# Three first weight chunks side by side instead of two, in a kernel that computes one hybrid attention and pooling layer

## What is computed

```
h = einsum('bsd,de->bse', x, w_in)                       # 2048 -> 9216 + 1024 + 1024 + 1024 + 4096
q, k, v, z_attn, u_pool, z_pool, g_pre = split(h, ...)
y_attn = (softmax-combined dilated attention of q, k, v) * silu(z_attn)
y_pool = causal_pool_mixer(u_pool, w_pool, pool_scale) * silu(z_pool)
merged = sigmoid(g_attn) * (y_attn @ w_proj_attn) + sigmoid(g_pool) * (y_pool @ w_proj_pool)
return layer_norm(2 ** 0.25 * x + merged @ w_out, ln_gamma, ln_beta)
```

## Time and profile before

| what | value |
|---|---|
| median of 3 runs | 961.87 us (961.44 to 961.93) |
| the profiled execution, its own time | 960.2 us |
| its span (first to last instruction) | 958.4 us |
| PE busy | 947.3 us, 99% of the span |
| PE weight loads (beside the matmuls) | 838.7 us |
| DVE busy | 633.7 us, 66% |
| ACT busy | 423.2 us, 44% |
| moved from HBM | 174.87 MB |

### The profile page before, as it was taken

One profiled execution on the slowest core, in us unless ns is written; L12 is line 12 of the kernel. 1 busy time (PEld: TensorE's weight loads), 2 busy tenths in 40 slices (PEclk: granted clock), 3 DMA queues, 4 the chain that ended last, 5 costly groups with the idle time before them and its releaser, 6 DMA issues.

```text
span 958.4 us, 14944 instructions
## 1 busy us (share of the span) xinstructions
PE 947.3 (99%) x5346; PEld 838.7 (88%) x5346; DVE 633.7 (66%) x996; ACT 423.2 (44%) x592; POOL 0.2 (0%) x4
## 2 busy tenths in 40 slices
PE   8999999999999999999999999999999999999996
PEld 6998898898898898898898899888888888888884
DVE  6767567567567567567567568666666666665666
ACT  6454354354354354354354354545445444543330
POOL 0000000000000000000000000000000000000000
PEclk9999999999999999999999999999999999999998
DMA  8744454445444445544444445655555554555532
GB/s 320 283 176 176 176 176 176 175 175 175 175 175 175 176 174 175 175 175 175 177 173 175 176 174 219 221 178 210 182 178 197 186 183 177 213 204 196 182 126 88
DMA packets 27543, 177.24 MB, mean 185 GB/s; under 512 B 3455, under 2 KB 4223, under 8 KB 7039
## 3 DMA queue, kind: packets, MB, share of 16 engines
q1 hardware_dynamic: 26928, 173.53, 50.1%
q10 hardware_dynamic: 596, 3.45, 1.0%
HBM read 174.87 MB, written 2.10 MB: 185 GB/s over the span
## 4 chain that ended last, share of the span: by engine, by line
PE 96%; DVE 1%; DMA 1%; SPq 1%; issue 0%; ACT 0%; DVEq 0%
PE proj_ps L337 40%; PE proj_ps L338 20%; PE attn_ps L337 6%; PE attn_ps L331 4%; PE attn_ps L332 4%; PE attn_ps L333 4%; PE attn_ps L338 3%; PE value_ps L332 3%; PE value_ps L333 3%; PE value_ps L331 3%; PE mixed_ps L445 1%; DMA w_raw<-in_weights 1%; PE mixed_ps L331 1%; PE mixed_ps L333 1%; PE mixed_ps L332 1%; PE attn_ps L406 1%
## 5 line engine op out<-in xcount | busy, mean ns | idle before, releaser
L337 PE MATMUL proj_ps<-xt,w_hi 128*128 128x512 f32 x1664 | 586.9, 397 | 1.8 <-DVE w_lo L756 1.0
L338 PE MATMUL proj_ps<-xt,w_lo 128*128 128x256 f32 x1664 | 466.9, 281 | 0.0
L727 DVE TENSOR_TENSOR w_lo<-w_raw,w_hi 128x1024 fp32r<-128x1024 f32 x318 | 374.2, 1220 | 81.5 <-ACT w_hi L576 80.1
L337 PEld LDWEIGHTS proj_ps<-xt,w_hi 128*128 128x128 f32 x1664 | 312.9, 188 | 76.3 <-DVE xt L749 1.5
L576 ACT ACTIVATE w_hi<-w_raw 128x1024 fp32r<-128x1024 f32 x318 | 318.3, 1051 | 54.1 <-PE mixed_ps L333 27.1
L338 PEld LDWEIGHTS proj_ps<-xt,w_lo 128*128 128x128 f32 x1664 | 315.0, 189 | 0.0
L595 ACT ACTIVATE corr<-proj_ps 128x256 f32<-128x256 f32 x104 | 39.9, 384 | 288.0 <-PE proj_ps L338 288.0
L741 DVE TENSOR_TENSOR qk_f<-proj_ps,corr 128x256 f32<-128x256 f32 x48 | 20.3, 424 | 79.0 <-ACT corr L595 79.0
L337 PE MATMUL attn_ps<-yp,w_hi 128*128 128x512 f32 x128 | 45.9, 397 | 0.0
L337 PE MATMUL attn_ps<-ya,w_hi 128*128 128x512 f32 x128 | 45.6, 396 | 0.0
L331 PE MATMUL attn_ps<-w_hi,xt 128*128 128x384 f32 x128 | 42.9, 335 | 0.0
(11 more groups left out here) (151 smaller groups left out, 884.4 us busy)
## 6 DMA issues: line engine op xcount, KB each, us to landing
w_raw<-in_weights SPq DMA_DIRECT2D x158, 1024.0 KB, 4.8
res<-in_x_rows ACTq DMA_DIRECT2D x1, 2048.0 KB
out_rows<-res SPq DMA_DIRECT2D x8, 256.0 KB, 2.2
xt_raw<-in_xt SPq DMA_DIRECT2D x3, 512.0 KB, 6.7
w_raw<-in_weights SPq DMA_DIRECT2D x6, 256.0 KB, 6.5
w_raw<-in_weights SPq DMA_DIRECT2D x2, 512.0 KB, 9.2
gamma<-in_gamma_row ACTq DMA_DIRECT2D x1, 1024.0 KB
mask<-in_mask SPq DMA_DIRECT2D x1, 576.0 KB, 4.4
```

The source lines that it names most:

```text
L337: mm(bank, w_hi[:, slot, cols], tile.rearrange("p a s -> p (a s)"), start=first, stop=False)
L338: return mm(bank[:, SEQ:2 * SEQ], w_lo[:, slot, cols], tile[:, 0, :], start=False, stop=last)
L727: tt(w_lo[:, slot, cols], w_raw[:, slot, cols], w_hi[:, slot, cols].bitcast(F32), ALU.subtract).then_inc(lo_split, 1)
```

## The change

PE works on chunks 0, 1 and 2 side by side, in bank 0 of `proj_ps`, in `value_ps` and in `mixed_ps` (both are first written otherwise much later in head 0). The weights of all three land in four pieces of four k-tiles; x keeps its five pieces. SP issues a piece of x and then the same piece of chunks 0, 1 and 2, where before the whole of chunk 2 came last. ACT issues three transfers of 256 KB in place of two of 128 KB. ACT and DVE split the pieces in the same order. In head 0, `next_bank` is left out for j = 0 to 2, and the split of chunk 2 is gone from the loop's lead-in. There are 11 warm-up matmuls instead of 8. The corresponding edits on DVE (`x_lo_part`, the loop over three chunks, the bank as an argument of `halves_summed`) mirror those on ACT.

```
-WARM_UP = 8
-
-PIECES = ((0, 2), (2, 4), (4, 8), (8, 12), (12, 16))
+WARM_UP = 11
+
+X_PIECES = ((0, 2), (2, 4), (4, 8), (8, 12), (12, 16))
+PIECES = ((0, 4), (4, 8), (8, 12), (12, 16))
+LAST = len(PIECES) - 1
...
+        def first_bank(n):
+
+            return (proj_ps[:, 0, :], value_ps[:, :], mixed_ps[:, :])[n]
+
+        def bank_of(j, first):
+            return first_bank(j) if first and j < RING else proj_ps[:, j % 2, :]
+
...
-        x_landed = [sem(f"x_landed{q}") for q in range(len(PIECES))]
+        x_landed = [sem(f"x_landed{q}") for q in range(len(X_PIECES))]
...
-        piece_landed = [[sem(f"piece_landed{n}_{q}") for q in range(len(PIECES) - 1)] for n in range(2)]
-        half_landed = sem("half_landed")
+        piece_landed = [[sem(f"piece_landed{n}_{q}") for q in range(LAST)] for n in range(RING)]
...
             load_x(0)
             load_x(1)
-            load_piece(0, 1)
-            load_piece(1, 1)
-            for q in range(2, len(PIECES)):
-                load_x(q)
-                load_piece(0, q)
-                load_piece(1, q)
-            for half, signal in enumerate((half_landed, raw_landed[2])):
-                cols = slice(half * HALF * P, (half + 1) * HALF * P)
-                sp.dma_start(w_raw[:, 2, cols], stream_d[2, :, cols]).then_inc(signal, 16)
+            for q in range(1, len(PIECES)):
+                load_x(q + 1)
+                for n in range(RING):
+                    sp.dma_start(w_raw[:, n, piece_cols(q)], stream_d[n, :, piece_cols(q)]).then_inc(
+                        piece_arrival(n, q), 16)
...
                 for q, (before, upto) in enumerate(PIECES):
-                    pe.wait_ge(x_lo_done, q + 1)
-                    for n in range(2):
+                    for n in range(RING):
                         if q == LAST:
                             pe.wait_ge(lo_split, 2 * n + 2)
                         else:
-                            pe.wait_ge(piece_lo_done, 2 * q + n + 1)
+                            pe.wait_ge(piece_lo_done, RING * q + n + 1)
                         for k in range(before, upto):
-                            bank, tile, first, last = from_x(n)(k)
-                            done = k_tile(bank, tile, n, k, first, last)
+                            x_piece = [start for start, _ in X_PIECES]
+                            if n == 0 and k in x_piece:
+
+                                pe.wait_ge(x_lo_done, x_piece.index(k) + 1)
+                            done = k_tile(first_bank(n), xt[:, k, :, :], n, k, k == 0, k == KT - 1)
...
-                    if first and j < 2:
+                    if first and j < RING:
                         if j == 0:
                             first_chunks()
...
-                    next_bank(0, j, i)
+                    if not first or j >= RING:
+                        next_bank(0, j, i)
...
-            for n in range(2):
+            for n in range(RING):
                 act.dma_start(w_raw[:, n, piece_cols(0)], stream_d[n, :, piece_cols(0)]).then_inc(
                     piece_landed[n][0], 16)
...
-            for q, (before, upto) in enumerate(PIECES):
+            def x_hi_part(q):
+                k = slice(*X_PIECES[q])
                 act.wait_ge(x_landed[q], 16)
-                activation(xt[:, before:upto, 0, :], xt_raw[:, before:upto, :], ACT.Copy).then_inc(x_hi_done, 1)
-                for n in range(2):
+                activation(xt[:, k, 0, :], xt_raw[:, k, :], ACT.Copy).then_inc(x_hi_done, 1)
+
+            x_hi_part(0)
+            for q in range(len(PIECES)):
+                if q > 0:
+                    x_hi_part(q + 1)
+                for n in range(RING):
                     act.wait_ge(piece_arrival(n, q), 16)
                     hi = activation(w_hi[:, n, piece_cols(q)], w_raw[:, n, piece_cols(q)], ACT.Copy)
...
-            for half, arrival in enumerate((half_landed, raw_landed[2])):
-                act.wait_ge(arrival, 16)
-                hi_part(2, half)
+                    if q == n == 0:
+                        x_hi_part(1)
...
-                    if not first or j > 0:
+                    if not first or j + AHEAD >= RING:
                         split_hi(0, j + AHEAD, i, A_CHUNKS)
...
-                        correction(0, j, i, A_CHUNKS)
+                        correction(0, j, i, A_CHUNKS, bank_of(j, first))

```

More of the change, by code:

```diff
@@ L252, in layer_kernel @@
         block = ctx.enter_context(nc.Block())
-        LAST = len(PIECES) - 1
         def piece_cols(q):
@@ L273, in load_x @@
             def load_x(q):
-                k = slice(*PIECES[q])
+                k = slice(*X_PIECES[q])
                 sp.dma_start(xt_raw[:, k, :], xt_d[:, k, :]).then_inc(x_landed[q], 16)
-            def load_piece(n, q):
-                sp.dma_start(w_raw[:, n, piece_cols(q)], stream_d[n, :, piece_cols(q)]).then_inc(
-                    piece_arrival(n, q), 16)
             load_x(0)
             load_x(1)
-            load_piece(0, 1)
-            load_piece(1, 1)
-            for q in range(2, len(PIECES)):
-                load_x(q)
-                load_piece(0, q)
-                load_piece(1, q)
-            for half, signal in enumerate((half_landed, raw_landed[2])):
-                cols = slice(half * HALF * P, (half + 1) * HALF * P)
-                sp.dma_start(w_raw[:, 2, cols], stream_d[2, :, cols]).then_inc(signal, 16)
+            for q in range(1, len(PIECES)):
[3 more added lines that the diff above has]
+                        piece_arrival(n, q), 16)
             sp.wait_ge(lo_split, 2)
@@ L584, in split_hi, with correction @@
                     hi_part((n + j) % RING, half)
-            def correction(n, j, i, per, pair=False):
+            def correction(n, j, i, per, bank=None, pair=False):
                 act.wait_ge(chunk_done, FROM + n + j + 1 + i * per)
@@ L593, in correction @@
                 else:
-                    b = (n + j) % 2
-                    activation(corr[:, b, :], proj_ps[:, b, SEQ:2 * SEQ], ACT.Copy).then_inc(act_evac, 1)
+                    activation(corr[:, (n + j) % 2, :], bank[:, SEQ:2 * SEQ], ACT.Copy).then_inc(act_evac, 1)
                 act.wait_ge(proj_free, FROM + banked(n, j) + i * banked_per(n))
-            for q, (before, upto) in enumerate(PIECES):
+            def x_hi_part(q):
+                k = slice(*X_PIECES[q])
                 act.wait_ge(x_landed[q], 16)
-                activation(xt[:, before:upto, 0, :], xt_raw[:, before:upto, :], ACT.Copy).then_inc(x_hi_done, 1)
-                for n in range(2):
+                activation(xt[:, k, 0, :], xt_raw[:, k, :], ACT.Copy).then_inc(x_hi_done, 1)
[4 more added lines that the diff above has]
+                for n in range(RING):
                     act.wait_ge(piece_arrival(n, q), 16)
@@ L671, in _ @@
                     split_hi(B_FIRST, j + AHEAD, i, B_CHUNKS)
-                    correction(B_FIRST, j, i, B_CHUNKS, pair=j % 3 == 2)
+                    correction(B_FIRST, j, i, B_CHUNKS, proj_ps[:, (B_FIRST + j) % 2, :], pair=j % 3 == 2)
                     if j % 3 < 2:
@@ L735, in split_lo, with halves_summed @@
                     lo_part(slot, half)
-            def halves_summed(dst, n, j, i):
+            def halves_summed(dst, n, j, i, bank):
                 dve.wait_ge(act_evac, banked(n, j) + 1 + i * banked_per(n))
-                tt(dst, proj_ps[:, (n + j) % 2, 0:SEQ], corr[:, (n + j) % 2, :], ALU.add).then_inc(proj_free, 1)
+                tt(dst, bank[:, 0:SEQ], corr[:, (n + j) % 2, :], ALU.add).then_inc(proj_free, 1)
             def freed(n, j, i):
@@ L746, in _, with x_lo_part @@
             nc.vector.memset(zeros[:, :].bitcast(F32), 0.0).then_inc(zeros_ready, 1)
-            for q, (before, upto) in enumerate(PIECES):
+            def x_lo_part(q):
+                k = slice(*X_PIECES[q])
                 dve.wait_ge(x_hi_done, q + 1)
-                tt(xt[:, before:upto, 1, :], xt_raw[:, before:upto, :], xt[:, before:upto, 0, :].bitcast(F32),
-                   ALU.subtract).then_inc(x_lo_done, 1)
-                for n in range(2):
+                tt(xt[:, k, 1, :], xt_raw[:, k, :], xt[:, k, 0, :].bitcast(F32), ALU.subtract).then_inc(x_lo_done, 1)
+            x_lo_part(0)
+            for q in range(len(PIECES)):
+                if q > 0:
+                    x_lo_part(q + 1)
+                for n in range(RING):
                     if q == LAST:
@@ L754, in _ @@
                     else:
-                        dve.wait_ge(piece_hi_done, 2 * q + n + 1)
+                        dve.wait_ge(piece_hi_done, RING * q + n + 1)
                     lo = tt(w_lo[:, n, piece_cols(q)], w_raw[:, n, piece_cols(q)],
@@ L761, in _ @@
                         lo.then_inc(piece_lo_done, 1)
-            split_lo(0, 2, 0, 0)
+                    if q == n == 0:
+                        x_lo_part(1)
             for pad in (u_pad, pool_a, pool_b):
@@ L846, in head @@
```

(10 more changed lines are left out.)

## The result

The changed kernel took 964.16 us (median of 10, 962.91 to 965.84), the kernel before 961.47 us in the same comparison: a ratio of 1.0029, 95% interval 1.0019 to 1.0039. Timed again later it took 963.17 us (median of 11) against 961.26, ratio 1.0023 (1.0014 to 1.0032). Forecast were 962.8 us and a range up to 964.0. The direction and the mechanism were right, the size was too small by a factor of two to three.

The account below looks back on a forecast made before the run. PE's work was taken to bound the kernel, with chunk 4's start deciding: issue of chunk 3 +1.96, start -0.3, spare time -0.69, so +0.97 us on the median of 961.87, giving 962.8 us, range 960.6 to 964.0.

Parts of the forecast that it names:

- What bounds the kernel; how much could be had: Whole kernel: PE's work is the total, only chunk 4's start counts for the end; 2.4 us gain at the very most.
- Part 1: First work: 11 warm-ups take 5.2 us, ending near 7.0 as the first weights are ready; 0 taken, not on the path.
- Part 2: Loads at the start: x's last piece lands behind 0.79 MB more, moving its split and SP's issue of chunk 3 by 1.96 us.
- Part 3: Start of the transfers: larger first pieces may bring x's last piece forward, 0 to 1.5 us; 0.3 taken.
- the sentence on interleaving: Start, in part 3: transfers from different engines share 16 DMA engines, so ACT's bytes delay the first real matmul up to 0.6 us.
- Part 4: Chunk 4: its load shifts 1.66 us, chunk 2's sum ends at 32.73, PE starts chunk 4 at 32.83, 0.97 us later.
- The wait doesn't bind: Rival, ahead of chunk 4: chunk 2's sum doesn't hold PE back; gain of 0.6 to 1.0 us, 960.9 to 961.3; 15%.
- all of it comes off: Rival: PE never short after 7.0 but for the first pieces; 1.8 to 2.4 us gained, 959.5 to 960.1; 5%.
- The clock's case: Rival: clock falls in PE's 2.0 us wait ahead of chunk 4, costing 1.7 us; +2.7, 964.5; 10%.
- The numbers: Whole kernel: +0.97 us added to the median of 961.87 gives 962.8; within 0.2% at 0.83, slower 0.12, faster 0.05.

Follow-up runs that it names:

- a3_small_first: Changed kernel with weights again in five pieces (2, 2, 4, 4, 4 k-tiles) for all three chunks and ACT's three transfers of 128 KB; 963.28 us, ratio 1.0021.
- a4_sp_third: Changed kernel with chunk 2's first piece issued by SP behind x's second piece, ACT issuing two 256 KB transfers instead of three; 964.22 us, ratio 1.0036.
- a6_all: Changed kernel with one sum waited for after chunk 3, tables issued behind chunk 5, and small first pieces (2, 2, 4, 4, 4 k-tiles); 962.81 us, ratio 1.0013.
- c3_after_times: The changed kernel itself, no edit, timed again with one execution profiled; median 963.17 us.
- c2_after_look: The changed kernel itself, no edit, run again for a third profile; the profiled execution took 963.2 us.

## Why the prediction fell short

- **What bounds the kernel; how much could be had.** Right: only chunk 4's start moved, and the rest of the span is the same to 0.1 us.
- **Part 1.** The 11 warm-ups took 4.16 us and not 5.2 (0.38 us each, where the eight before took 0.47), so they ended at 5.99 and not near 7.0. Real work began at 7.85, not at 7.0: x's first piece was split at 5.84 instead of 4.6, and the larger piece of weights behind it. After the wait of 1.86 us between the two the clock fell, to 0.50 from 8.5 to 11.5, so chunks 0 to 2 ended at 26.35 and not at 25.2 at the latest. That it isn't on the path was right: PE still waited 1.40 us for chunk 3.
- **Part 2.** +1.96 us on x's last piece. With small pieces in both, the four profiles with three chunks side by side (mean 15.81) against the three with the old transfers (13.44, 14.13, 14.72: 14.10) give 1.7 us, close to the term. There the transfers bind: in `a3_small_first` ACT waited 0.65 us for x's last piece and DVE 0.28 us for ACT. In the changed kernel they aren't alone in it: DVE has no idle time from 11.61 to 20.5. It took up x's last piece at 17.56, just as it was done with the pieces ahead of it, and three pieces of chunk 2 (0.63 us each) now stand ahead of chunk 0's last, so an earlier landing alone would have helped little. The prediction moved the chain behind that piece along and did not count DVE's work.
- **Part 3 is the step that failed.** "I take 0.3", with bounds from 0 to 1.5 us of gain and none on the side of a loss. The start became slower: 163 GB/s in place of 229 from 2 to 5.5, and 1.06 us more on x's last piece in the pair of profiles than part 2 gives, so the term was -0.3 where this pair has +1.06. Part of that is the one profile of before, whose x's last piece was split 0.7 to 1.3 us earlier than in two others with the same transfers. By the means with three chunks side by side (16.34 against 15.81) the larger pieces cost 0.5 us. Why equal bytes in larger first pieces move more slowly is not shown; that the size matters is. By the sentence on interleaving, the Trainium skill, "DMA: Bandwidth & Descriptors", section "Issuing engines are not separate DMA queues", x's first pieces are slowed by ACT's bytes. They were 1.23 us later in the pair of profiles, but 5.25 and 5.48 in the two others with the old transfers are hardly earlier than 5.39 to 5.84 in the changed kernel; with one transfer of ACT fewer (`a4_sp_third`) x's first piece was no earlier; and the rule says nothing of the lower total rate.
- **Part 4.** The chain was right in its links: 3.79 us from ACT's start on chunk 4 to the end of chunk 2's sum forecast, 3.79 measured (30.65 to 34.44). The tables are the second term with a wrong size: they cost 4.19 us of SP instead of 3.22, for one issue of 1.40 us. From SP's issue of chunk 4 to ACT's start on it were 7.05 us, against 7.67 before. Of the 1.66 us between the forecast 32.83 and 34.49, the start makes 1.36 (16.46 against 15.10), the tables 0.97, the shorter way of chunk 4 takes off 0.62, and PE's start behind the sum 0.05.
- **The rivals.** "The wait doesn't bind" and "all of it comes off" didn't come true. The clock's case was real but misplaced: it falls ahead of chunk 3, after waits of 2.19 and 2.39 us, in the variants with small pieces (`a6_all` and `a3_small_first`). The 10% for it stood on a wait of 2.0 us ahead of chunk 4, which was 0.5 to 1.1.
- **The numbers.** The median of the other executions added 1.7 us to the profiled time. That set the level at 961.87, of three executions; ten have 961.47, so 0.4 us of the 962.8 brought it nearer to the result by chance. The shift was taken from one profile with an early start, which the sum could not see. Measured from median to median it is 1.9 to 2.7 us, not 0.97.

## What to carry to other kernels

Feeding more chunks side by side delays the release of every buffer among them; follow the next load from that release before counting the idle time saved. Where a wait counts completions in order, ask which single one it needs: here a sum that the bank did not need carried a late load to PE. And take the start of a program from more than one profile, or give its terms a bound on the side of a loss too.

## What the runs showed that was not expected

- The start of the transfers differs between executions of the same first transfers: x's last piece was split at 13.44, 14.13 and 14.72 in three profiles. The changed kernel's four lie within 0.21 us.
- One of SP's issues near 20 to 23 us took 1.2 to 2.0 us instead of 0.43 in three of the four profiles of the changed kernel, and none did in the fourth, nor in the three with the old transfers (0.52 us at most). What holds it up isn't in the trace.
- The granted clock fell to 0.50 at the beginning of the changed kernel in two of its four profiles: after a wait of 1.86 us that followed 4.2 us of warm-up, and in `c3_after_times` after waits of 1.06 and 0.57 us with 1 us of work between them. In `c2_after_look` waits of 1.06 and 0.30 us left it up. Ahead of chunk 3 it fell in two profiles, after waits of 2.19 and 2.39 us that followed some 13 us of dense work; it did not fall there after waits of 1.40 to 2.04 us in five, nor in that of `a4_sp_third` with 2.61 us. So the length of the wait alone does not decide it. `c3_after_times`, with a granted clock of 0.50 from 9 to 12:

```profile
7.40 0.50 PE L335 MATMUL proj_ps<-xt,w_hi 128*128 128x512 f32 x1 [1.06 <-DVE w_lo L766]
...
8.94 0.78 PE L335 MATMUL proj_ps<-xt,w_hi 128*128 128x512 f32 x1 [0.57 <-DVE xt L755]
```
